# Prompt attention of a hybrid decoder step: scores computed transposed, four heads at a time, with the row maximum from a separate one-pass product

## The chip, the core and the metric

The kernel runs on one core of one Trainium2 chip. The metric is the device time of one execution in microseconds (us), the median of several runs. Engines are named as the profile names them: PE is TensorE (matrix products), PEld its weight loads, DVE VectorE, ACT ScalarE, POOL GpSimd, SP the queue that issues most DMAs.

## What is computed

One layer of a decoder is run for a prompt of 1024 tokens and for 8 requests of one new token each. The part that changes is the prompt's attention with three branches. There are 8 heads of 64 values, in 2 groups of 4 heads that share keys and values; queries are handled in blocks of 128.

```python
def masked_softmax(s, mask):
    s = jnp.where(mask, s.astype(jnp.float32), NEG)
    m = jnp.max(s, axis=-1, keepdims=True)
    p = jnp.where(mask, jnp.exp(s - m), 0.0)
    return p / jnp.maximum(jnp.sum(p, axis=-1, keepdims=True), 1e-30)
...
s = jnp.einsum('bqgrd,bngd->bqgrn', qg, kv_cmp[:, :, 0]).astype(jnp.float32) * ATTN_SCALE
s = s - slopes[:, :, None] * dist[None, :, None, None, :]
...
o = g[..., 0:1] * o_c + g[..., 1:2] * o_s + g[..., 2:3] * o_w
```

Each branch is scores, a distance term with a slope for each head, a mask, a softmax, and a product with the values. Branch 0 (selected) sees all earlier tokens, since with 1024 tokens all 16 blocks are selected. Branch 1 (window) sees the last 512. Branch 2 (compressed) sees 63 summary positions. The three outputs are added with sigmoid gates.

## The kernel before

The program is one hand-written stream for each engine, with semaphores between them. The order on PE is: input turned and projected (to 169 us), prompt attention (169.7 to 468.4 us), decode attention, recurrence, merge, and the feed-forward part, which takes half the time. Nothing else is on PE during the prompt attention, so that stage lies in the span as a whole.

Products of queries and keys are done with split operands (a high part and a low part in the type fp32r) so that they come near to full precision. One product over 128 rows takes the high keys twice against high and low queries (`k_high_twice`, `q_high_low`, L1008), a second over 65 rows takes the low keys against the high queries and the slope against the positions (L1010).

The stage is 128 jobs `j`: for each pair of heads, each block of queries `i` (0 to 7), and for `wc` 0 (selected) or 1 (window and compressed), each of the two heads. In a job:

- PE `scores`: queries are the weights and keys move, up to 512 columns at a time, so that the result has one query in each partition. Masks are added by a product of the identity and a bf16 mask (L1012, L1019).
- DVE `maxima` (L2029, L2035) takes the negated maximum over the row; ACT `exp` (L1634, L1640) takes the exponential with it as bias and sums the row in the same pass.
- PE `turn` (L1036) turns the probabilities, 128 keys at a time; ACT (L1666) and DVE `second` (L2067) copy them out of the accumulator memory.
- PE `pv` (L1056), for both heads of a pair in turn: the values are the weights, 64 columns wide, one head in each half of the array, and 128 probabilities move. The operands are plain fp32, which the trace records as two instructions for each product.
- ACT `parts` (L1648), PE `turn_parts` (L1065), DVE `scaled_sum` (L2053, L2055), PE `turn_sum` (L1070) and ACT `out` (L1653) scale by gate over sum, add the branches and turn the result back.

Four banks of the accumulator memory hold scores, two hold turned probabilities, and two hold outputs.

## Time and profile before

| | |
|---|---|
| median of 3 runs | 2190.33 us (2186.76 to 2195.27) |
| profiled execution, first to last instruction | 2191.0 us |
| PE busy | 2114.1 us, 96% of the span |
| DVE busy | 1035.5 us, 47% |
| ACT busy | 703.1 us, 32% |
| prompt attention (first L1008 to the last ACT copy) | 169.7 to 468.4 us, 298.7 us |

The profiled execution and the median agree within 0.7 us. Busy time counts an instruction from its start to its modelled end, so that overlapping products count once; the view of the chain of work shows what each one adds.

### The profile page before, as it was taken

How to read it: one execution, taken by the hardware profiler on the slowest of the kernel's cores; microseconds unless marked ns; L12 is line 12 of the kernel's file. 1: busy time of each engine (PE TensorE's matmuls, PEld its weight loads, DVE VectorE, ACT ScalarE, POOL GpSimd, SP SyncE). 2: the span in 40 equal slices, each digit the busy share in tenths (PEclk: the TensorE clock that was granted, in tenths of full speed). 3: DMA queues.
4: the chain of work that ended last, by engine and by line, in shares of the span. 5: the costliest groups of instructions: out<-in, count | busy, mean ns of one | idle time of the engine just before them, and what ended most of it. 6: DMA issues, size and time to landing. Idle time of an engine off the chain costs nothing.

```text
span 2191.0 us, 33624 instructions
## 1 busy us (share of the span) xinstructions
PE 2114.1 (96%) x14200; PEld 1827.4 (83%) x14200; DVE 1035.5 (47%) x1889; ACT 703.1 (32%) x1358; POOL 162.9 (7%) x164
## 2 busy tenths in 40 slices
PE   8999999989979999999999999999999999999997
PEld 7997777758639999999888886789888998889985
DVE  2136666636442466767221225644444344444447
ACT  3226677735431344444111112121111122111222
POOL 0021000001110122221000000000000000000007
PEclk9998999999999999999999999999999999999999
DMA  9322000135573222221321204121111111111101
GB/s 225 109 71 104 11 2 11 49 124 198 180 252 108 49 61 59 57 61 42 106 58 30 58 20 135 39 86 40 49 39 50 48 48 49 39 39 58 39 20 78
DMA packets 140626, 158.91 MB, mean 73 GB/s; under 512 B 25842, under 2 KB 122315, under 8 KB 135612
## 3 DMA queue, kind: packets, MB, share of 16 engines
q1 hardware_dynamic: 132444, 113.98, 17.3%
q0 software_dynamic: 8032, 42.78, 6.3%
q8 instruction: 113, 1.85, 0.3%
q14 instruction: 37, 0.30, 0.0%
HBM read 141.16 MB, written 19.76 MB: 73 GB/s over the span
## 4 chain that ended last, share of the span: by engine, by line
PE 89%; DMA 3%; DVE 3%; ACT 2%; issue 1%; SPq 0%; DVEq 0%; ACTq 0%; POOLq 0%
PE PS L834 62%; PE PS L1423 5%; PE PS L1056 3%; PE PS L1036 3%; PE PS L1139 3%; DMA arena<-in_cache_sel_kv,arena 2%; PE PS L1008 2%; PE PS L1010 1%; PE PS L1124 1%; PE PS L1349 1%; PE PS L1515 1%; PE PS L1065 1%; DMA arena<-in_x_prompt 1%; PE PS L1477 1%; PE PS L1292 1%
## 5 line engine op out<-in xcount | busy, mean ns | idle before, releaser
L834 PE MATMUL PS<-x_low,w_high_mlp 128*128 128x344 f32 x1056 | 338.1, 320 | 0.0
L834 PE MATMUL PS<-w_down_high,hidden 128*128 128x512 f32 x960 | 308.2, 395 | 0.9 <-DVE w_down_low L2547 0.9
L834 PE MATMUL PS<-x_high,w_low 128*128 128x344 f32 x768 | 246.1, 320 | 0.0
L2541 DVE TENSOR_TENSOR arena<-arena,PS 128x512 f32<-128x512 f32 x244 | 167.4, 687 | 134.9 <-PE PS L834 134.7
L834 PE MATMUL PS<-x_high,w_high_mlp 128*128 128x344 f32 x720 | 230.3, 320 | 0.0
L834 PEld LDWEIGHTS PS<-w_down_high,hidden 128*128 128x128 f32 x960 | 180.1, 188 | 54.3 <-DVE arena L2541 12.0
L834 PE MATMUL PS<-w_down_low,hidden 128*128 128x512 f32 x512 | 200.9, 392 | 0.0
L834 PEld LDWEIGHTS PS<-x_low,w_high_mlp 128*128 128x128 f32 x1056 | 198.6, 188 | 2.7
L834 PE MATMUL PS<-x_low,w_high_hgrn 128*128 128x344 f32 x600 | 192.6, 321 | 0.0
L834 PE MATMUL PS<-x_high_a,w_low 128*128 128x344 f32 x480 | 154.1, 321 | 0.0
L834 PE MATMUL PS<-x_high_b,w_low 128*128 128x344 f32 x468 | 149.7, 320 | 0.0
L834 PEld LDWEIGHTS PS<-x_high,w_low 128*128 128x128 f32 x768 | 144.5, 188 | 0.0
L834 PEld LDWEIGHTS PS<-x_high,w_high_mlp 128*128 128x128 f32 x720 | 135.8, 189 | 2.1 <-issue 1.5
L1576 ACT ACTIVATE arena<-PS 128x344 f32<-128x344 f32 (+1 forms) x105 | 47.9, 458 | 265.3 <-PE PS L834 265.2
L1893 ACT ACTIVATE w_down_high<-arena 128x2048 fp32r<-128x2048 f32 x15 | 28.7, 1916 | 275.2 <-PE PS L834 275.2
L1423 PE MATMUL PS<-arena,wring 128*128 128x344 f32 x384 | 114.7, 452 | 1.2 <-issue 1.2
L834 PEld LDWEIGHTS PS<-x_low,w_high_hgrn 128*128 128x128 f32 x600 | 113.8, 190 | 0.0
L834 PEld LDWEIGHTS PS<-w_down_low,hidden 128*128 128x128 f32 x512 | 96.1, 188 | 21.1
L858 DVE TENSOR_TENSOR w_low<-wring,w_high_mlp 128x1024 fp32r<-128x1024 f32 x44 | 53.6, 1219 | 108.9 <-ACT w_high_mlp L852 108.9
L834 PE MATMUL PS<-x_high_a,w_high_hgrn 128*128 128x344 f32 x300 | 102.0, 340 | 1.3 <-DMA x_high_b<-x_high_kept 1.3
L2701 POOL TENSOR_TENSOR arena<-arena 128x1024 f32<-128x1024 f32 (+1 forms) x8 | 19.6, 2451 | 1102.8 <-ACT arena L1905 1102.8
L1423 PEld LDWEIGHTS PS<-arena,wring 128*128 128x128 f32 x384 | 72.1, 190 | 35.1 <-issue 1.4
(390 smaller groups left out, 4285.0 us busy)
## 6 DMA issues: line engine op xcount, KB each, us to landing
wring<-in_w_in SPq DMA_DIRECT2D x100, 256.0 KB, 3.4
wring<-in_w_up SPq DMA_DIRECT2D x64, 256.0 KB, 3.2
arena<-in_w_down SPq DMA_DIRECT2D x16, 1024.0 KB, 5.0
arena<-in_x_prompt SPq DMA_DIRECT2D x16, 512.0 KB, 3.9
x_high_kept<-x_high_att SPq DMA_DIRECT2D x1, 4128.0 KB, 14.4
arena<-in_cache_win_kv SPq DMA_DIRECT2D x8, 512.0 KB, 4.5
arena<-in_w_out SPq DMA_DIRECT2D x2, 2048.0 KB, 8.8
out<-in_cache_win_kv SPq DMA_DIRECT2D x1, 4088.0 KB
```

What stands on the lines that cost most here:

```text
L834: mm = pe.matmul(out, w, x, start=(start and k == 0 and i == 0), stop=(stop and k == tiles - 1 and i == 2))
L858: dve.tensor_tensor(wl[:, n % WR, :, 0:m], wring[:, n % WR, :, 0:m], high[:, :, 0:m].bitcast(F32), ALU.subtract).then_inc(wl_dve, 1)
L1008: pe.matmul(out, qa, k1[g][:, br, k0:k0 + n], start=True, stop=False)
L1010: mm = pe.matmul(out, qb, k2[br][g][0:65, k0:k0 + n], start=False, stop=True)
L1036: mm = pe.transpose(PS[0:n, 4 + turned % 2, P * b:P * (b + 1)], probs(j, col, n), ident)
L1056: mm = pe.matmul(PS[HD * two:HD * (two + 1), 6 + i % 2, c:c + P], v[0:r, :], PT[(2 * n + two) % 3][0:r, b // 4, P * (b % 4):P * (b % 4 + 1 ...
L1065: mm = pe.transpose(PS[:, 6 + n % 2, P * a:P * (a + 1)], out_parts(n)[:, P * a:P * (a + 1)], ident)
L1139: mm = pe.matmul(PS[:, 4 + 2 * (b % 2) + c, 0:256], cw2[:, c, 4 * half + q, :], xt2[:, n % 2, 256 * (4 * c + q):256 * (4 * c + q + 1)], st ...
L1423: mm = pe.matmul(PS[:, product_bank(s, ab), 0:cn], wring[:, n % WR, 4 * ab + k, :], a[:, k, c0:c0 + cn], start=(k == 0), stop=(k == 3))
L1576: act.activation(dst[0:m, c0:c0 + cn], unit_out(3 * n + ci, m, cn), fn).then_inc(u_act, 1)
L1893: act.activation(wdh[:, :, :], wdn[:, g % 2], ACT.Copy).then_inc(wdh_act, 1)
L2541: dve.tensor_tensor(y, y, PS[:, 5 + d % 3, :], ALU.add).then_inc(dn_dve, 1)
```

## The change

The stage becomes 16 jobs `n`, one for each group of four heads and block of queries; the second group takes the blocks from 7 down to 0. A job has one step for each block of keys: `i + 1` selected, up to 5 window, 1 compressed, which makes 148 steps in all. In a step:

- PE `scores(n, x)`: 128 keys are the weights and the queries of four heads move, 512 columns, so that the result has one key in each partition. Two fp32r products as before (128 rows, and 68 rows that hold the low queries against the high keys, the slope and the three negated maxima). Where a mask is needed, the mask is the weight and the identity moves four times (512 columns).
- ACT `exp(n, x)`: one exponential of 512 columns with no bias and no row sum, straight into the weights of the next product.
- PE `values(s)`, two steps behind: for each head, the 128 x 128 probabilities are the weights, and 64 values and a column of ones move, 65 columns. The last column gives the row sum.

The maximum must be known ahead of the scores. `bound_scores(n + 1, p)` computes the next job's scores once more in the old layout, with one fp32r product over 65 rows (high parts alone) and the old masks, in 8 to 16 pieces, which take turns in two banks; DVE `bound` reduces each piece; PE `turn_max` turns the maxima and ACT `max_rows` puts them in as three rows of the queries. The pieces are spread over the steps of job `n`, all but the last two. After a job DVE `branch_sum` does sums, gates and the sum over branches in five steps, and PE `turn_out` turns it with two transposes.

The transposes of probabilities (`turn`), their copies (L1666, L2067), `parts` and `turn_parts` are gone. POOL sets ones, zeros and slopes ahead of the stage. The values are stored in rows of 65, and go out in four DMAs in place of two. The DMA that keeps the output runs once for each group (2 in place of 4).

```diff
+        def keys(n):
+            i = job(n)[1]
+            return [(0, b) for b in range(i + 1)] + [(1, b) for b in range(max(0, i - 4), i + 1)] + [(2, 0)]
...
+        def pieces(n):
+            i = job(n)[1]
+            w, lo = P * (i + 1), P * max(0, i - 4)
+            if i < 3:
+                return [[(0, 0, w, 0)], [(1, 0, w, 0), (2, 0, NCMP_P, w)]]
+            if i == 3:
+                return [[(0, 0, 512, 0)], [(1, 0, 512, 0)], [(2, 0, NCMP_P, 0)]]
+            return [[(0, 0, 512, 0)], [(0, 512, w - 512, 0)], [(1, lo, 512, 0)], [(1, lo + 512, P, 0), (2, 0, NCMP_P, P)]]
...
+        def pieces_at(n, x):
...
+            steps, total = len(keys(n)) - 2, 4 * len(pieces(n + 1))
+            return range(total * min(x, steps) // steps, total * min(x + 1, steps) // steps)
...
+            def bound_scores(n, p):
+                g, i = job(n)
+                hh, piece = p // len(pieces(n)), pieces(n)[p % len(pieces(n))]
+                x = first_piece[n] + p
...
+                if x >= 2:
+                    pe.wait_ge(sp_dve, x - 1)
+                q = q3[n % 2][0:HD + 1, P * hh:P * (hh + 1)]
+                for br, k0, w, col in piece:
+                    k = kc2[0:HD + 1, g, :] if br == 2 else k2[br][g][0:HD + 1, k0:k0 + w]
+                    mm = pe.matmul(PS[:, x % 2, col:col + w], q, k, start=True, stop=True)
...
+                        mm = pe.matmul(PS[:, x % 2, c:c + m.shape[1]], mask("ident"), m, start=False, stop=True,
...
+                mm.then_inc(sp_ps, 1)
...
+            def turn_max(n):
+                pe.wait_ge(m_dve, n + 1)
+                ring_free("max", n)
+                for hh in range(4):
+                    mm = pe.transpose(PS[0:HD + 4, ring_bank("max", n), P * hh:P * (hh + 1)], mx[:, 4 * hh:4 * hh + HD + 4], ident)
+                mm.then_inc(rb_ps, 1)
...
+            def scores(n, x):
...
+                out = PS[:, ring_bank("scores", n, x), :]
+                if br == 2:
+                    ka, kb, r = kc1[:, g, :], kc2[0:HD + 4, g, :], NCMP_P
...
-                    pe.matmul(out, qa, k1[g][:, br, k0:k0 + n], start=True, stop=False)
...
-                    mm = pe.matmul(out, qb, k2[br][g][0:65, k0:k0 + n], start=False, stop=True)
...
-            def turn(j, gi):
...
-                    mm = pe.transpose(PS[0:n, 4 + turned % 2, P * b:P * (b + 1)], probs(j, col, n), ident)
...
-            def pv(n):
...
-                        mm = pe.matmul(PS[HD * two:HD * (two + 1), 6 + i % 2, c:c + P], v[0:r, :],
-                                       PT[(2 * n + two) % 3][0:r, b // 4, P * (b % 4):P * (b % 4 + 1)],
...
+                    ka, kb, r = k1[g][:, br, P * b:P * (b + 1)], k2[br][g][0:HD + 4, P * b:P * (b + 1)], P
+                pe.matmul(out[0:r, :], ka, q1[n % 2][:, :], start=True, stop=False)
+                mm = pe.matmul(out[0:r, :], kb, q2[n % 2][0:HD + 4, :], start=False, stop=True)
+                m = mask("cmpmask", CMP_BACK - 8 * i) if br == 2 else mask("causal") if b == i else None
+                if br == 1 and b == i - 4:
+                    m = mask("winlow")
+                if m is not None:
+                    mm = pe.matmul(out.rearrange("p (h q) -> p h q", h=4), m, mask("ident").unsqueeze(1).to_broadcast([P, 4, P]),
+                                   start=False, stop=True, skip_group_check=True)
+                mm.then_inc(rb_ps, 1)
...
+            def values(s):
+                n, x = step_of[s]
+                g, i = job(n)
+                br, b = keys(n)[x]
+                pe.wait_ge(rb_act, ring["scores", n, x] + 1)
...
+                for hh in range(4):
+                    c = (HD + 2) * (3 * (hh % 2) + (br + 1) % 3)
+                    mm = pe.matmul(PS[:, 4 + 2 * (n % 2) + hh // 2, c:c + HD + 1], PT[:, s % 4, P * hh:P * (hh + 1)], v,
+                                   start=(x == 0 and hh % 2 == 0), stop=(br == 2 or b == i), skip_group_check=True)
...
+            for p in range(first_piece[1]):
+                bound_scores(0, p)
+            turn_max(0)
+            for n in range(NJ):
+                for x in range(len(keys(n))):
+                    scores(n, x)
+                    if n and x == out_step(n):
+                        turn_out(n - 1)
+                    for p in pieces_at(n, x):
+                        bound_scores(n + 1, p)
+                    if first_step[n] + x >= 2:
+                        values(first_step[n] + x - 2)
+                    if n + 1 < NJ and x == len(keys(n)) - 2:
+                        turn_max(n + 1)
+            for s in range(first_step[NJ] - 2, first_step[NJ]):
+                values(s)
+            turn_out(NJ - 1)
...
+            def max_rows(n):
+                act.wait_ge(rb_ps, ring["max", n] + 1)
+                act.activation(q2[n % 2][HD:HD + 4, :], PS[HD:HD + 4, ring_bank("max", n), :], ACT.Copy).then_inc(rb_act, 1)
+            def exp(n, x):
+                s, r = first_step[n] + x, NCMP_P if keys(n)[x][0] == 2 else P
+                act.wait_ge(rb_ps, ring["scores", n, x] + 1)
+                if s >= 4:
+                    act.wait_ge(pv_ps, s - 3)
+                act.activation(PT[0:r, s % 4, :], PS[0:r, ring_bank("scores", n, x), :], ACT.Exp).then_inc(rb_act, 1)
...
+                for at, (br, k0, w, col) in enumerate(piece):
+                    second = br < 2 and k0 == (512 if br == 0 else P * max(0, i - 4) + 512)
+                    dst = mx2[:, hh, br:br + 1] if second else mxr[:, hh, 1 + br:2 + br]
+                    ins = dve.tensor_reduce(dst, PS[:, x % 2, col:col + w], AX.X, ALU.max, negate=True)
...
+            def branch_sum(n):
...
+                dve.wait_ge(pv_ps, first_step[n + 1])
+                steps(dve.tensor_scalar(f, o[:, :, :, HD], 1e-30, None, ALU.max))
+                steps(dve.reciprocal(f, f))
+                steps(dve.tensor_tensor(f, f, gates[:, i, 12 * g:12 * g + 12].rearrange("p (a c) -> p a c", a=2), ALU.mult))
+                steps(dve.tensor_tensor(parts, o[:, :, :, 0:HD], f.unsqueeze(3).to_broadcast([P, 2, 6, HD]), ALU.mult))
+                dve.tensor_reduce(osum[:, n % 2, :, :], parts.rearrange("p a (t br) d -> p (a t) d br", br=3), AX.X, ALU.add
```

Where the instructions stand now. On PE, at the block of queries 6, before: two selected jobs of the pair, with the transposes between scores and products (each `L1056 64x128` row is one product, that is two instructions of the trace).

```order
L1008 MATMUL PS<-k_high_twice_54,q_high_low_61 128x512
L1010 MATMUL PS<-k_low_56,q_high_63 128x512
L1008 MATMUL PS<-k_high_twice_54,q_high_low_61 128x384
L1010 MATMUL PS<-k_low_56,q_high_63 128x384
L1012 MATMUL PS<-masks 128x128
L1036 MATMUL PS<-consts_sb,arena 128x128 x5
L1036 MATMUL PS<-consts_sb,arena 64x128
L1056 MATMUL PS<-arena 64x128 x12
```

On PE after, in job 6 (block 6 of the first group): three selected steps, with pieces of job 7 between `scores` (L1042, L1043) and `values` (L1064).

```order
L1042 MATMUL PS<-q_high_twice_61,k_high_low_53 128x512
L1043 MATMUL PS<-q_low_rows_65,k_high_rows_55 128x512
L1005 MATMUL PS<-k_high_rows_55,q_high_slope_64 128x512
L1064 MATMUL PS<-arena 128x65 x4
L1042 MATMUL PS<-q_high_twice_61,k_high_low_53 128x512
L1043 MATMUL PS<-q_low_rows_65,k_high_rows_55 128x512
L1005 MATMUL PS<-k_high_rows_55,q_high_slope_64 128x512
L1012 MATMUL PS<-masks 128x128
L1005 MATMUL PS<-k_high_rows_57,q_high_slope_64 128x512
L1012 MATMUL PS<-masks 128x128
L1064 MATMUL PS<-arena 128x65 x4
```

The transposes are gone from between the two kinds of product, the product with the values takes full-width weights, and the maximum's products stand in their place.

On PE after, at the start of the stage: the last piece of job 0, the turned maxima (L1024), the first scores, and the first pieces of job 1.

```order
L1005 MATMUL PS<-kc_high_rows,q_high_slope_63 128x64
L1012 MATMUL PS<-masks 128x64
L1024 MATMUL PS<-consts_sb,arena 68x128 x4
L1042 MATMUL PS<-q_high_twice_61,k_high_low_53 128x512
L1043 MATMUL PS<-q_low_rows_65,k_high_rows_55 128x512
L1048 MATMUL PS<-masks 128x512
L1005 MATMUL PS<-k_high_rows_55,q_high_slope_64 128x256
L1012 MATMUL PS<-masks 128x128
```

Before, the scores of the first five jobs stood here without a maximum ahead of them; now the first `scores` stand behind `turn_max(0)`, which waits for DVE and is followed by a copy on ACT.

On DVE before, in the same region of the stage: short reductions and copies by turns.

```order
L2029 TENSOR_REDUCE arena<-PS 128x1
L2035 TENSOR_REDUCE arena<-PS 128x1
L2067 COPY arena<-PS 128x384
L2043 RECIPROCAL arena<-arena 128x6
L2045 TENSOR_TENSOR arena<-arena 128x6
L2029 TENSOR_REDUCE arena<-PS 128x1
L2035 TENSOR_REDUCE arena<-PS 128x1
L2067 COPY arena<-PS 128x384
L2035 TENSOR_REDUCE arena<-PS 128x1
L2067 COPY arena<-PS 128x128
```

On DVE after, around the end of a job: the low queries (L1974), two or three reductions (L2010), then `branch_sum` (L2026 to L2030) and the reductions that PE's next pieces wait for.

```order
L1974 SCALAR_TENSOR_TENSOR q_low_rows_65<-arena,q_high_twice_61 64x2x128 x2
L2010 TENSOR_REDUCE arena<-PS 128x1 x3
L2026 TENSOR_SCALAR arena<-PS 128x12
L2027 RECIPROCAL arena<-arena 128x12
L2028 TENSOR_TENSOR arena<-arena 128x12
L2029 TENSOR_TENSOR arena<-PS,arena 128x768
L2030 TENSOR_REDUCE arena<-arena 128x256
```

The five instructions of `branch_sum` stand as one block between reductions; PE's pieces reuse their two banks only behind it.

## Rows read from the trace of the kernel before

**Rows 1.** The page: engines, and the chain that ended last by engine.
```profile
PE 2114.1 (96%) x14200; PEld 1827.4 (83%) x14200; DVE 1035.5 (47%) x1889; ACT 703.1 (32%) x1358; POOL 162.9 (7%) x164
...
PE 89%; DMA 3%; DVE 3%; ACT 2%; issue 1%; SPq 0%; DVEq 0%; ACTq 0%; POOLq 0%
```

**Rows 2.** Busy us of each engine by stretch, granted clock (PEclk), DMA share, GB/s.
```profile
core 0: us, PE busy (x) PEld busy (x) DVE busy (x) ACT busy (x) POOL busy (x), PEclk, DMA share, GB/s
...
169.70:188.00 18.30, 17.30 (x94) 13.02 (x95) 11.81 (x29) 12.52 (x46) 2.01 (x2) 0.56 0.58 218
188.00:462.00 274.00, 262.16 (x2513) 206.29 (x2513) 174.28 (x439) 194.75 (x577) 0.00 (x0) 0.99 0.05 18
```

**Rows 3.** What TensorE waited for from 169.7 to 468.4 us: total, times, longest.
```profile
PE PS L1056 <- ACT arena L1666: 4.5, 3, 1.5
...
PE PS L1036 <- ACT arena L1666: 0.3, 1, 0.3
```

**Rows 4.** TensorE by line and shape, same stretch: count, busy us, mean ns.
```profile
L1036 PE MATMUL PS<-consts_sb,arena 128*128 128x128 f32 x528 | 83.0, 283 | 1.8 <-DVE arena L2067 1.0 <-ACT arena L1666 0.3
L1056 PE MATMUL PS<-arena 128*64 128x128 f32 x1056 | 73.1, 282 | 6.6 <-ACT arena L1666 4.5 <-DVE arena L2067 1.3
L1008 PE MATMUL PS<-k_high_twice,q_high_low 128*128 128x512 f32 x88 | 42.9, 487 | 1.8 <-ACT arena L1640 1.8
```

**Rows 5.** Chain of work 278 to 285 us: start, us on the chain, what.
```profile
278.48 1.39 PE PS L1056 x20
279.87 0.43 PE PS L1008
280.30 0.24 PE PS L1010
280.54 0.07 PE PS L1012
280.61 0.12 PE PS L1008
...
281.00 0.11 PE PS L1018
...
281.15 0.58 PE PS L1036 x5
...
283.25 1.24 PE PS L1056 x20
```

**Rows 6.** The same chain at 1039 us, in the recurrence (full-width products, 64 columns).
```profile
1038.95 0.64 PE PS L834 x4
1039.59 0.84 PE PS L1292 x8
1040.43 0.53 PE PS L834 x3
1040.96 0.84 PE PS L1292 x8
```

**Rows 7.** The same chain at 770 us (8-column weights, 64 columns moved).
```profile
769.98 0.99 PE PS L1284 x16
```

**Rows 8.** VectorE by line and shape, 169 to 469 us (same columns).
```profile
L2055 DVE TENSOR_REDUCE arena<-arena 128x128 f32<-128x384 f32 x32 | 19.0, 594 | 1.1
L2053 DVE TENSOR_TENSOR arena<-PS,arena 128x384 f32<-128x384 f32 x32 | 17.8, 557 | 41.4 <-PE PS L1065 41.4
L2029 DVE TENSOR_REDUCE arena<-PS 128x1 f32<-128x64 f32 x64 | 14.1, 220 | 39.5 <-PE PS L1019 39.3
...
L2035 DVE TENSOR_REDUCE arena<-PS 128x1 f32<-128x512 f32 x16 | 11.0, 685 | 8.3 <-PE PS L1012 8.3
...
L2035 DVE TENSOR_REDUCE arena<-PS 128x1 f32<-128x256 f32 x16 | 6.6, 415 | 6.6 <-PE PS L1012 6.6
...
L2035 DVE TENSOR_REDUCE arena<-PS 128x1 f32<-128x128 f32 x16 | 4.3, 287 | 2.1 <-PE PS L1012 1.8
```

**Rows 9.** ScalarE by line and shape, 155 to 469 us (same columns).
```profile
L1666 ACT ACTIVATE arena<-PS 128x512 f32<-128x512 f32 x80 | 48.1, 601 | 57.7 <-PE PS L1036 57.3
```

586 lines of the change are left out of this document (243 added, 343 removed).

## The prediction

> **What bounds the kernel now.** I read the page first. PE is busy 96% of the span, and 89% of the chain that ended last is PE [rows 1]. PE is one in-order stream with nothing beside the prompt attention, so whatever this stage gains or loses on PE reaches the end. The stage is 298.7 us, from the first L1008 at 169.7 to the last copy at 468.4.
>
> Next, the stretches. From 188 to 462 us PE is busy 262 of 274 us, DVE 174, ACT 195 [rows 2]. So PE bounds the stage too, but 4% of it is idle, and both helpers have room. The first 18.3 us run at a granted clock of 0.56, nearly all of it at the lower of TensorE's two levels (1.2 GHz), although PE is busy 17.3 us of them [rows 2]. The granted clock fell after PE had waited for the last projection copy and the first maxima. The waits of PE in the stage have nine causes, from 4.5 us down to 0.3 us, together 14.5 us [rows 3].
>
> Busy time of overlapping products doesn't price them. The chain of work does: it shows what each adds. An fp32r product of 512 columns adds 0.23 us, one of 128 columns 0.12, one of 64 columns 0.11, a mask of 128 columns 0.07, a transpose 0.58 / 5 = 0.116 [rows 5]. A product with the values is two instructions in two halves of the array; two groups of 20 instructions take 1.39 and 1.24 us, so I take 0.066 each. Leaving the halved array costs too: the L1008 behind it adds 0.43 in place of 0.23 [rows 5].
>
> **Does this price list give the stage as it is?** Score products: each head has 11 spans of 512 columns, 3 of 384, 3 of 256, 7 of 128 and 8 compressed ones of 64, and each span is done twice. 88 x 0.233 + 24 x 0.18 (between its neighbours) + 24 x 0.12 + 56 x 0.12 + 64 x 0.11 = 41.4 us, twice 82.8. Masks 160 x 0.07 + 64 x 0.04 = 13.8. Transposes 592 x 0.116 = 68.7 (528 of them in [rows 4], the rest 64 columns wide). Value products 1184 x 0.066 = 77.9 (1056 of them in [rows 4]). Leaving the halves 64 x 0.17 = 11. Turning the outputs, 128 x 0.116 = 14.8. The sum is 269. With 14.5 of waits and 8 for the low clock (18.3 x 0.44) it is 292, against 298.7 measured: 2% short. The list can be used.
>
> **What the change removes.** All 592 transposes of probabilities (68.7 us), the old value products (77.9), leaving the halves (11), and 96 of the output transposes (11).
>
> **What it adds, on PE.**
> - Scores: 148 steps of two products of 512 columns, 296 x 0.233 = 69.0 us, in place of 82.8.
> - Score masks: in 56 steps, 512 columns. No row has this form; 0.07 for 128 columns and another 384 at the slope between 128 and 512 columns (0.113 for 384) gives 0.18, the sum of both ends at most 0.07 + 0.233 = 0.30. I take 0.24: 13.4 us.
> - The maximum's product: one of the two products of before, 41.4 us, with the old masks, 13.8 us.
> - Value products: 592, now with full-width weights and 65 columns moved, so 1184 instructions. This is the term that decides. The nearest row is L1292, a product of the same type with 128 x 128 weights and 64 columns: 8 instructions add 0.84 us, and the three L834 behind them add 0.53 where four add 0.64, 0.16 each, elsewhere; so (0.84 + 0.05) / 8 = 0.111 us each [rows 6]. L1284 moves the same 64 columns with 8-column weights at 0.99 / 16 = 0.062 [rows 7]. So it isn't the moved columns that cost 0.111; it is the full-width weights, loaded anew for each instruction. The new products load new probabilities each time. 1184 x 0.111 = 131.4 us. The bounds are 0.062 (73 us) and 0.116, a transpose (137 us).
> - Turned maxima and outputs: 96 x 0.116 = 11.1 us.
> - Narrow results: 16 compressed steps give 64 keys only. If each costs what the halves cost to enter and leave (up to 0.3), 5 us; nothing at the low end.
>
> The sum is 69.0 + 13.4 + 41.4 + 13.8 + 131.4 + 11.1 + 5 = 285. The same sum for before was 269. So what the 592 transposes and the halved products cost (158 us with leaving) nearly comes back as 131 for the new ones and 55 for the maximum. On PE work alone the change loses 16 us. It has to win that back from waits.
>
> The Trainium skill has a rule that speaks here: "TensorE: Matmul & The Clock Gate", section "LDWEIGHTS (loading the stationary operand)", says that a load takes its number of columns divided by 1.2 in ns, whatever the rows. For 128 columns that is 107 ns, and the trace's 0.111 agrees. By that rule swapping weights and moved operand trades a 64-column load for one of 128 columns that 65 moved columns can't cover.
>
> **What waits are left.** Today's waits (14.5) go with their instructions. New ones:
> - Start. Today the first scores run at once. Now eight pieces of job 0 go first, and DVE takes 4 x (0.287 + 0.287 + 0.220) = 3.2 us for them [rows 8] where PE needs 2.1. Then come a DVE step (0.2), the turn and its latency (0.3 over its price), and the copy of 512 columns on ACT, 0.6 [rows 9]. Job 0 has one step for the eight pieces of job 1: DVE 4 x (0.415 + 0.415 + 0.220) = 4.2 against 2.1 [rows 8]. That is about 4.5 us idle. The low clock stays, and does its harm to the PE work in it only: 6 us. Together 10 (bounds 8, as today, and 16 if the idle start keeps the clock low for longer).
> - Middle. DVE has 100 pieces for each group. Reductions sum to 114 us by their means (0.685 for 512 columns, 0.287 for 128 [rows 8]), `branch_sum` 16 x 2.5, of which its two large steps are 1.0 each (0.557 and 0.594 for half the columns [rows 8], and 0.4 more), low queries 16 x 0.7. Together 165 of 285 us: DVE isn't the bound. But `branch_sum` blocks it for 2.5 us, and PE can be two pieces ahead. A step of PE is 0.47 scores + 0.89 values + pieces. Where a step has 1.3 pieces (large blocks) PE meets the block after two steps, 3 us: hidden. Where it has 2.3 (jobs 2 to 4) it waits about 1 us. I take 5 us in all.
> - ACT: an exponential of 512 columns is 0.6 to 0.7, the copies of queries 0.7 more in the first two steps; a PE step is 1.4 or more, and PE reads the result two steps later. Hidden. If it weren't, each step would cost the difference.
> - End. `branch_sum` of the job before last stands in a job of three steps, and that of the last job has nothing ahead of it: 2.5 - 0.7, then 2.5, and a turn and a copy (0.9): 5 us.
>
> POOL's ones and slopes end before the projections do, and its larger DMAs leave during the stage, when the DMA share is 0.05 [rows 2]: nothing. If that cover were gone, the copies of 1 to 2 us would show at 169.7 us.
>
> Stage: 285 + 10 + 5 + 5 = 305, and 2 for the shortfall of the list: 307, that is 8 us more than 298.7. The profiled execution was 2191.0, the median 2190.3; so about 2199 us.
>
> **Rivals.**
> - Forecast: the stage is 299 to 313 us, the time 2190 to 2205. PE work as priced, waits of 14 to 28 us. Chance 0.50.
> - The pieces' two banks bind. There are 200 pieces, and each waits for the reduction two before it. PE to DVE and back costs some 0.1 to 0.2 us that no price holds, and if it shows on each piece, that is 20 us more, 2205 to 2222 (say 2218). For it: DVE is the slower side per piece (0.685 for 512 columns against 0.23 on PE). Against it: 1.4 us of other PE work lies between the pieces of large blocks. It decides once a piece's round trip is over the step. Chance 0.22.
> - Other side, mild: the waits vanish. The start is hidden behind the clock's return, DVE is never late, narrow results cost nothing. The stage is 280 to 292 us, 2172 to 2185. Against: today's deeper buffers still leave 14.5 us. It turns into a gain once start, middle and end together stay under 13 us. Chance 0.22.
> - Other side, large: the weight loads are hidden. If a new value product costs 0.062, as with narrow weights [rows 7], 1184 x 0.049 = 58 us go, 2141 us. For it: loads and products overlap elsewhere (the 344-column products, full width too, add 0.16 [rows 6]). Against: L1292 is the same form, and adds 0.111. The point at which the whole change breaks even is 0.104. Chance 0.06. The same page of the Trainium skill (section "Step-by-step: what each phase is for") has the next loads pulled ahead so that they run during a product; by that alone the product would cost its moved columns, as this rival has it, and rows 6 against rows 7 show that it doesn't for 64 columns.
>
> **Numbers.** Two runs of this kernel can't be told apart under 0.5%, 11 us: faster is below 2179.4, slower above 2201.3. Faster: 0.06 and 0.07 of the mild case, 0.13. Slower: 0.15 of the forecast and all of the second case, 0.37. Same: 0.50. The range holds the forecast, most of the second case and half of the mild one: 2180 to 2217. The forecast's own is 2190 to 2205.
>
> **What the profile after would show.** If I am right: L1064 adds 0.11 us an instruction on the chain, 131 us together; PE idle in the stage is 10 to 20 us, most of it at either end behind DVE L2010 and L2030; DVE is busy about 165 us there, ACT under 150; the granted clock is near 0.5 for the first 15 to 25 us of the stage and full behind. Wrong if L1064 adds 0.06 (large gain), if PE waits for L2010 throughout (loss of 20 us or more), or if a product of 512 columns with 68 rows, or the mask with a repeated identity, costs far from 0.23.

## The result, and the profile after

The changed kernel takes 2238.5 us (median of four runs; three at 2230.6 to 2242.7), the kernel before 2188.6 on the same chip: the ratio is 1.022, 95% interval 1.019 to 1.025. I had forecast 2199 (2180 to 2217), so the forecast was 40 us too low and the time is outside the range. The fourth run, at 2302.4 us with a mean granted clock of 0.941, is left out of the ratio, as two runs of one experiment (e6_nomax, 2187.7 and 2189.3 us) are. The median of the other three is 2234.3; below, an experiment is compared with this one, while the recorded expectations compare with 2238.5. The profiled execution took 2242.7, with a span of 2240.8.

The stage now reaches from 172.3 to 518.8 us: 346.5 us, 48 more than before. The windows of the changed kernel show where (the same columns as [rows 2]):

```profile
core 0: us, PE busy (x) PEld busy (x) DVE busy (x) ACT busy (x) POOL busy (x), PEclk, DMA share, GB/s
172.00:188.00 16.00, 12.99 (x61) 9.04 (x62) 7.08 (x27) 3.73 (x7) 8.70 (x14) 0.65 0.59 165
188.00:235.00 47.00, 41.04 (x256) 31.60 (x254) 26.91 (x70) 26.90 (x50) 0.00 (x0) 0.90 0.17 73
235.00:293.00 58.00, 58.00 (x232) 47.92 (x230) 18.36 (x41) 14.10 (x26) 2.02 (x2) 0.50 0.00 1
293.00:462.00 169.00, 166.72 (x1208) 139.49 (x1207) 82.64 (x189) 78.37 (x148) 0.00 (x0) 1.00 0.04 13
462.00:519.00 57.00, 51.05 (x366) 42.20 (x366) 26.44 (x70) 24.40 (x49) 0.00 (x0) 0.93 0.05 19
```

Look at the third row. For 58 us PE is busy all the time, at a granted clock of 0.50, which is the lower level of 1.2 GHz. It runs 232 products there, 4.0 in a microsecond; in the row behind, at the full clock, 1208 in 169 us, 7.1. Before, the clock was 0.99 from 188 to 462 us [rows 2]. The trace's record of the clock has the changed kernel at the lower level in four stretches up to the stage's end: from 177.0 for 13.7 us, from 217.9 for 6.8, from 235.0 for 58.0, and from 511.5 for 17.1. Before, it has them from 172.1 for 17.1 us, from 260.8 and from 332.5 for 3.4 each, and, just behind the stage, from 469.0 for 10.2. The two of 3.4 stand behind waits of 1.5 us for L1666, and a third wait of 1.5 us, at 404.7, has none behind it. So in the old stream a wait of this length cost little by the clock.

What PE waited for in the stage (total, times, longest):

```profile
PE PS L1005 <- DVE arena L2010: 9.0, 13, 2.1
PE PS L1072 <- DVE arena L2030: 4.9, 2, 2.8
PE PS L1042 <- ACT q_low_rows L1638: 0.9, 1, 0.9
PE PS L1024 <- DVE arena L2018: 0.7, 1, 0.7
PE PS L1005 <- ACT arena L1579: 0.5, 1, 0.5
PE PS L1107 <- ACTq L1675: 0.5, 1, 0.5
```

Together 16.5 us, against 14.5 in [rows 3]. The waits don't explain 48 us.

The chain of work of the changed kernel in three places: ahead of the long stretch (from 231 us), within it (253 us) and after it (330 us):

```profile
231.65 0.97 DVE arena L2029
232.62 0.02 issue
232.65 1.03 DVE arena L2030
233.68 0.61 DVE arena L2010
234.29 0.04 issue
234.33 0.50 PE PS L1005
234.83 1.35 PE PS L1064 x8
...
252.31 0.43 PE PS L1043
252.74 0.45 PE PS L1048
253.19 1.60 PE PS L1064 x8
254.80 0.53 PE PS L1042
...
330.65 0.89 PE PS L1064 x8
331.55 0.28 PE PS L1042
331.83 0.24 PE PS L1043
332.07 0.23 PE PS L1048
```

At the full clock eight value instructions add 0.89 us, 0.111 each, as priced. The mask of 512 columns (L1048) adds 0.23, priced 0.24. At the low clock each of these costs 1.8 to 2 times as much. Ahead of the stretch DVE does `branch_sum` (L2029 and L2030, 2.0 us) and only then the piece's maximum (L2010). PE waited 1.8 us for it and went on at 234.33. At 235.0 the clock fell. The fall at 217.9 stands behind a wait of 2.1 us that ended at 217.2, in which DVE did most of `decode_queries` (the queries of the decode part, 1.7 us), with a `branch_sum` just ahead of it.

**How much is clock, how much is work?** A run's span times its mean granted clock is about the time that it would take at the full clock throughout, since PE bounds nearly all of it; the rest, span x (1 - clock), is lost to the low clock. Before (seven runs beside the first experiments): clock 0.984 to 0.988, so 26 to 35 us lost and 2156 to 2159 without them. After: 0.968, 0.975 and 0.973, so 72, 56 and 60 us lost, and 2169 to 2177 without them. So 10 to 21 us of the loss are work and waits, where 8.7 were forecast, and the other 30 or so are the clock (63 us lost on average against 30).

### The profile page after: what moved, and what is told of

It is laid out like the page before. It is cut to its first block, busy times and chain, and to the rows that moved or that the text cites. A ratio compares the mean times of both kernels' runs of the same rounds, so it can differ in the third digit from the quotient of the medians.

```text
span 2240.8 us, 31835 instructions
## 1 busy us (share of the span) xinstructions
PE 2165.8 (97%) x13672; PEld 1882.4 (84%) x13672; DVE 1004.5 (45%) x1807; ACT 641.8 (29%) x1010; POOL 169.8 (8%) x178
## 4 chain that ended last, share of the span: by engine, by line
PE 91%; DVE 4%; DMA 3%; issue 1%; ACT 1%; SPq 0%; DVEq 0%; ACTq 0%; POOLq 0%
PE PS L841 60%; PE PS L1064 6%; PE PS L1426 5%; PE PS L1142 2%; PE PS L1005 2%; PE PS L1042 2%; DMA arena<-in_cache_sel_kv,arena 2%; PE PS L1043 2%; PE PS L1127 1%; PE PS L1352 1%; DVE arena L2010 1%; PE PS L1518 1%; PE PS L1048 1%; DMA arena<-in_x_prompt 1%; PE PS L1012 1%
## 5 line engine op out<-in xcount | busy, mean ns | idle before, releaser
L2010 DVE TENSOR_REDUCE arena<-PS 128x1 f32<-128x512 f32 (+4 forms) x256 | 104.3, 445 | 171.2 <-PE PS L1012 105.8
L1064 PE MATMUL PS<-arena 128*128 128x65 f32 x1184 | 170.9, 292 | 0.0
L1064 PEld LDWEIGHTS PS<-arena 128*128 128x128 f32 x1184 | 166.5, 212 | 2.9
L1645 ACT ACTIVATE arena<-PS 128x512 f32<-128x512 f32 (+1 forms) x148 | 88.3, 597 | 168.6 <-PE PS L1043 91.8
```

The costliest lines, as they stand in the source:

```text
L1064: mm = pe.matmul(PS[:, 4 + 2 * (n % 2) + hh // 2, c:c + HD + 1], PT[:, s % 4, P * hh:P * (hh + 1)], v, start=(x == 0 and hh % 2 == 0), sto ...
L1645: act.activation(PT[0:r, s % 4, :], PS[0:r, ring_bank("scores", n, x), :], ACT.Exp).then_inc(rb_act, 1)
L2010: ins = dve.tensor_reduce(dst, PS[:, x % 2, col:col + w], AX.X, ALU.max, negate=True)
```

## The experiments

Two theories at first. Both are about why the clock stays low while PE is busy. **Theory A**: PE's work in this stage moves few columns for the weights that it loads (65 columns for 128 loaded, twice over for each product), and where little moves, a low clock is held though PE is busy. **Theory B**: only the waits count; whatever makes PE wait for DVE costs the clock, and what the products look like is of no matter. Each wants an edit that leaves the other's cause as it is.

**e2_wide.** Each value product moves 128 columns (both groups' values) in place of 65. The weight loads and the number of instructions stay. What this kernel computes is no longer the prompt attention: columns of neighbours are added together, and the lower limit of the row sum is 1.0 in place of 1e-30.

```diff
-                v = vcN[:, g, :] if br == 2 else kvV[:, b, br, g, :]
+                v = (vcN if br == 2 else kvV[:, b, br, :, :]).rearrange("p g d -> p (g d)")[:, 0:128]
...
-                    mm = pe.matmul(PS[:, 4 + 2 * (n % 2) + hh // 2, c:c + HD + 1], PT[...], v,
+                    mm = pe.matmul(PS[:, 4 + 2 * (n % 2) + hh // 2, c:c + 128], PT[...], v,
```

> The changed kernel, but each value product moves 128 columns (64 values, ones, and the first 63 of the other group's) in place of 65; the attention output is not the reference's (neighbouring columns are added together, and the lower limit of the sum is 1.0). At the full clock it costs PE nothing if the full-width weight load bounds the product (0.111 us an instruction with 65 columns; 128 columns of a plain fp32 product add 0.11 too). Theory A (the low granted clock makes the loss, and few moved columns behind long weight loads hold it there): the 58 us stretch at the low clock with PE busy disappears or shrinks to under 20 us, the time falls by 15 to 35 us, to about 2205 to 2220. Theory B (waits for DVE start the low clock and nothing in the products holds it): the clock falls as before, same time within 10 us, 2230 to 2245. Theory C (the products bind by their moved columns): 30 us or more slower.

Measured: 2213.7 us, ratio to before 1.011 (1.008 to 1.014). Twice the columns, and 21 us faster. The waits for L2010 are as they were. The window from 200 to 450 us (columns as above), first of the changed kernel, then of this one:

```profile
200.00:450.00 250.00, 242.43 (x1534) 200.77 (x1532) 117.70 (x274) 106.91 (x199) 2.02 (x2) 0.87 0.03 13
```

```profile
200.00:450.00 250.00, 241.71 (x1730) 201.04 (x1730) 128.00 (x299) 119.78 (x224) 2.02 (x2) 0.99 0.03 10
```

Its PE waits for the maxima in the stage:

```profile
PE PS L1005 <- DVE arena L2010: 9.4, 14, 2.1
```

And a step of its chain of work:

```profile
303.16 0.95 PE PS L1064 x8
304.11 0.23 PE PS L1042
304.34 0.23 PE PS L1043
```

Two things follow. The granted clock is 0.99 where it was 0.87, with the waits unchanged: theory B alone falls. The same two waits are there, of 2.1 us (to 215.1) and 1.8 us (to 230.6); behind the first the clock is low for 3.4 us, behind the second not at all. And eight instructions with twice the columns add 0.95 with 0.23 behind them, in place of 0.89 and 0.28, the same sum to 0.01. The moved columns were hidden behind the weight loads: the price of 0.111 is that of the weights.

**e3_thin.** The same edit with 32 columns in place of 128, so that half of the values and the row sums are left out.

> The changed kernel, but each value product moves 32 columns in place of 65; the attention output is not the reference's (half the values and the sums are left out, and the lower limit of the sum is 1.0). Theory A: L1064 still adds 0.11 us an instruction at the full clock, the stretches at the low clock grow (over 80 us in the stage), and the time rises by 10 to 60 us, to 2245 to 2300. Theory B: no change, 2230 to 2245. Theory C: the products get cheaper by up to half, 50 us faster, about 2185.

Measured: 2430.6 us, ratio 1.112 (1.108 to 1.116): half the columns, 196 us slower. The clock is at the lower level for 491 us on end, from 196.3 to 687.8, nearly all of a stage that now lasts until 704. From 200 to 450 us PE is busy 249 of 250 us, and waits for L2010 are down to 1.9 us in the whole stage:

```profile
200.00:450.00 250.00, 249.15 (x968) 204.58 (x967) 79.23 (x185) 71.35 (x133) 2.02 (x2) 0.50 0.01 5
```

That is theory A at its clearest: PE busy 99.7% and the clock not given back. The stretch starts 2.5 us behind a wait of 0.45 us, at 193.8; the changed kernel has the same wait, at 198.3, and keeps its clock.

**e5_spread.** PE's program stays as changed; DVE's isn't. `branch_sum` is split over three steps, and `decode_queries`, `low_k` and ACT's copies of the second group's keys move to jobs with more steps.

```diff
-                    if x == 2 and n:
+                    if 2 <= x < 5 and n and len(keys(n)) > 5:
+                        branch_sum(n - 1, x - 2)
+                    if x == 2 and n and len(keys(n)) <= 5:
                         branch_sum(n - 1)
-                    if n == 2 and x == 3:
+                    if n == 5 and x == 5:
                         decode_queries()
```

> The changed kernel with DVE's work spread: the five steps of the branch sum stand in three consecutive steps of the job (where it has more than five), and the decode queries and the second group's low keys with their ACT copies are made in jobs 5 and 6 in place of 2 and 3. PE's stream is unchanged. Theory A and B both expect the waits of L1005 for L2010 to fall from 9 us to 4 or less. Theory B: the falls of the clock at 218 and 235 us are gone, the time falls by 25 to 40 us, to 2195 to 2212. Theory A: fewer falls, but one that does come is held as long; the time falls by 5 to 35 us. If only the waits count (theory D, DVE lateness is the whole loss), the time falls by about 5 us and the clock stays as it is.

Measured: 2211.5 us, ratio 1.010 (1.007 to 1.013), 23 us better than the changed kernel. The waits of PE for DVE in the stage fell from 9.0 to 2.9 us for the maxima, and rose from 4.9 to 7.5 behind the split sum (now L2033). Its 2.8 us stand at the end of the stage; between 190 and 470 us no wait is longer than 0.65 us:

```profile
PE PS L1072 <- DVE arena L2033: 7.5, 9, 2.8
PE PS L1005 <- DVE arena L2010: 2.9, 7, 0.7
```

And its window from 200 to 450 us:

```profile
200.00:450.00 250.00, 245.50 (x1776) 203.27 (x1775) 129.61 (x310) 124.27 (x233) 2.02 (x2) 1.00 0.03 10
```

That is 3.5 us less waiting, and span times clock is 2169, at the lower end of the changed kernel's 2169 to 2177. What went is the low clock in the middle: 1.00, where the changed kernel has 0.87 in the same window. So the falls at 218 and 235 us need their long waits. With the stream as changed a wait starts the fall, and the few moved columns make it last.

**e6_nomax.** The maximum's products, masks and reductions are left out, with a constant bound in place of the maximum, so that small probabilities vanish.

> The changed kernel without the maximum: bound_scores and its reductions are left out, and a constant stands for the negated maximum, so small probabilities vanish and the output is not the reference's. PE loses 55 us of products and masks by the price list, and the waits of L1005 for DVE (9 us). If the clock stays near full behind the start: 2170 + 0 - 55 - 10 + 20, about 2130 to 2150. If the low clock is held by the value products (theory A), their share of PE grows, and low stretches of 50 us or more remain: 2150 to 2185. Theory B: no waits, so no low clock behind the first 20 us: 2125 to 2140.

Measured: 2129.0 to 2142.1 us in three runs, ratio 0.976 (0.971 to 0.980); span times clock is 2100 to 2102. So the maximum costs about 68 us of the changed kernel's 2169. PE's own price was 41.4 + 13.8 = 55, and the 9.0 us of waits for the maxima went too; the 4 us left weren't looked for. The three runs lie where theory B had them (2125 to 2140, one run 2 us above), not where theory A had (2150 to 2185), at a clock of 0.982 to 0.988. So theory A's first form, in which value products of 65 columns hold the clock low whatever PE waits for, missed: even a stream in which they have a larger share can keep its clock where PE seldom waits. No trace shows the stage in these three runs.

**e7_both.** e5_spread and e2_wide together.

> Both edits together: DVE's sum over the branches is spread over three steps and its other long blocks are moved, and each value product moves 128 columns in place of 65 (so the output is not the reference's). Theory A (a fall of the clock needs a PE wait, and it lasts because value products move few columns behind full-width weights): either edit alone already took away the 65 us at the low clock in the middle of the stage, so together they don't add up; what is left of the low clock in the stage is its start and its end. The wide one alone gave 2213.7, the spread one alone 2211.5; together 2195 to 2207, since the waits (9.4 against 2.9 us) go as well. Rival (the two edits take away two different losses, 25 and 27 us): 2185 to 2190.

Measured: 2205.3 us, ratio 1.007 (1.005 to 1.009). The two gains (21 and 23 us) don't add up, since together they bring 29; in the main they take away the same loss. The clock is 0.983 to 0.986, near before's. What is left over before is 16.5 us, most of it the change's own cost in work and waits (span times clock is 2170 to 2173).

**e9_thin_more.** e3_thin, with the first score product of each step issued twice. A third theory stands against A here, **rival C**: the form of the value products alone decides, not what PE moves in all.

```diff
+                pe.matmul(out[0:r, :], ka, q1[n % 2][:, :], start=True, stop=True)
                 pe.matmul(out[0:r, :], ka, q1[n % 2][:, :], start=True, stop=False)
```

> The kernel whose value products move 32 columns in place of 65 (2430.6 us, clock held low for 491 us; the output is not the reference's), with more work: the first score product of each of the 148 steps (512 columns, fp32r, 0.233 us at the full clock) is issued twice, its first result overwritten. Added PE work 34 us at the full clock, 66 at the low. Theory A (the low clock is held where little moves behind the weight loads, so more moved columns let it come back): the clock returns, 2205 to 2250, that is about 200 us faster with 34 us more work. Rival C (what holds the clock is the value products' form or the stage itself, not what the engine moves in all): 2480 to 2500.

Measured: 2405.9 us, ratio 1.099 (1.097 to 1.101). More work, and 25 us faster than e3_thin, but the clock is still low for 324 us (from 240.3) and in three shorter stretches ahead of it. Both expectations missed in size, theory A's by over 150 us. The sign is theory A's: rival C wanted 50 us more.

**e8_r1 and e10_r1_wide.** Probabilities and values in fp32r (lower precision of this product), so that one instruction of 66 columns takes the place of two of 65; then the same with 128 columns (again with columns of neighbours added together).

```diff
-        PT = view(o, 4, 512); o += 4 * 512
+        PT = view(o, 4, 512)
+        PTr = rounded("probs_rounded", arena_at, o, 4, 512); o += 4 * 512
...
-                    mm = pe.matmul(PS[..., c:c + HD + 1], PT[:, s % 4, P * hh:P * (hh + 1)], v,
+                    mm = pe.matmul(PS[..., c:c + HD + 2], PTr[:, s % 4, P * hh:P * (hh + 1)], v,
```

> Probabilities and values stored as fp32r, so each value product is one instruction of 66 columns in place of two of 65 (592 in place of 1184). This lowers the precision of that product. It tests two terms: the price of a value product (0.111 us an instruction, by its weights), and the clock. If an fp32r value product also adds 0.11 us, 592 x 0.111 = 66 us go from the time without the low clock's loss (2169): 2103, and with the 30 us of loss at the stage's ends 2130 to 2145. Theory A by moved columns over time: a full step moves 1024 + 264 columns in about 0.90 us, more for each us than the changed kernel (1024 + 520 in 1.36), so the clock is held low no longer than there: 2130 to 2165. Rival C (what counts is the moved columns per weight load of the value products alone): low for most of the stage, 2250 to 2320.

> As the fp32r value products, but each moves 128 columns in place of 66 (the output is not the reference's). If the weight load sets the price of a value product, nothing is added, 0.11 us each: 2103 without loss, and with the loss at the ends 2130 to 2140, whichever theory of the clock holds. If the 66-column kernel is at 2130 to 2145 too, moved columns of the value products matter neither to price nor clock there; if it is far slower and this one isn't, rival C holds.

Measured: 2295.3 us (1.048, 1.046 to 1.050) with 66 columns, 2221.0 (1.016, 1.012 to 1.021) with 128. Removing 592 instructions made the kernel 61 us slower. Span times clock fell from 2169 to 2093, that is 0.128 us for each instruction removed (0.111 for itself, the rest for what stood around it). But the clock is low for 341 us on end, from 211.0. Rival C had this time right (2250 to 2320), and theory A had not (2130 to 2165). Doubling the columns gives 74 us back, which is rival C's way too, and the low stretches are then 7 to 21 us long, though there are many: its clock is 0.945 to 0.956, below the changed kernel's. The window of e8_r1 from 200 to 450 us:

```profile
200.00:450.00 250.00, 245.64 (x914) 189.18 (x912) 99.62 (x230) 89.40 (x166) 2.03 (x2) 0.52 0.03 9
```

The same window of e10_r1_wide:

```profile
200.00:450.00 250.00, 233.96 (x1170) 176.97 (x1168) 121.83 (x288) 114.00 (x216) 2.02 (x2) 0.75 0.03 9
```

My reading of theory A for e8_r1 was wrong: I had counted its moved columns as if fp32 and fp32r instructions were alike, and by this count it moves more in each microsecond than the changed kernel. It behaves as if it moved less. The trace of before has the time for a plain fp32 instruction of 256 columns with full-width weights, in the decode part:

```profile
499.92 3.47 PE PS L1139 x16
```

That is 0.217 us each, 0.85 ns a column, where an fp32r product of 512 columns takes 0.23 [rows 5], 0.45 ns a column. So an fp32 instruction occupies PE nearly twice as long for each column, and 128 of them, as in e2_wide, last just as long as the load (0.11). If fp32 columns are counted twice, the changed kernel moves slightly more than e8_r1, and the order of the kernels fits in the main, though not throughout (see the table). That the clock goes by such a count is an inference; no run tests it apart.

**e11_r1_more.** e8_r1 with the first score product of each step issued twice.

> The kernel with fp32r value products of 66 columns (2295.3 us, held at the low clock for 341 us; value products at fp32r precision), with more work: the first score product of each step (512 columns) is issued twice, its first result overwritten: 148 x 0.233 = 34 us more at the full clock, 66 more at the low one. Theory A, as the last runs left it: the low clock is held where columns move in too small a part of the time, each fp32 instruction counting its columns twice; the stream then stands between the fp32r kernel with 66 columns (held 341 us) and the one with 128 (2221.0, held 10 to 20 us at a time). So the clock comes back from time to time, and the kernel gets faster by work that it doesn't need: 2180 to 2250. Rival C (the value products alone decide): 2330 to 2360.

Measured: 2239.0 us, ratio 1.020 (1.015 to 1.025): 148 needless products of 512 columns make the kernel 56 us faster. Span times clock rose by 47 (34 were priced, so this measure is off by some 10 us where the clock is low for long), and the clock rose from 0.907 to 0.915 up to 0.955 to 0.967. Rival C, by which the value products alone decide, falls: they are the same here, and it wanted 2330 to 2360. Its window from 200 to 450 us, beside e8_r1's 0.52:

```profile
200.00:450.00 250.00, 241.59 (x1132) 185.53 (x1130) 109.74 (x258) 99.44 (x185) 2.02 (x2) 0.72 0.03 9
```

**e12_r1_spread.** e8_r1 with e5_spread's program for DVE.

> The fp32r kernel with the spread sum and the moved blocks on DVE, so with few PE waits (value products at fp32r precision). Its time without the low clock's loss is 2093. Theory B (the clock falls only behind a wait of PE, however little moves): it stays full from about 190 us on, 2115 to 2130, which would be faster than before by 3%. Theory A' (where little enough moves the clock falls and stays low by itself, waits or not): 2260 to 2300, hardly changed. The kernel with 32 columns had few waits left and was held for 491 us, so I hold A' for likelier.

Measured: 2288.3 us, ratio 1.045 (1.041 to 1.048), 7 us from e8_r1. The waits for the maxima are down to 2.7 us, six times, longest 0.8, and the clock is low all the same: for 95.6 us from 211.8, behind the wait of 0.8, and for 228.7 us from 317.6, behind one of 1.6 us for the last step of the sum. Those two waits, and then the window from 200 to 450 us:

```profile
PE PS L1006 <- DVE arena L2011: 2.7, 6, 0.8
PE PS L1073 <- DVE arena L2034: 1.6, 1, 1.6
```

```profile
200.00:450.00 250.00, 246.64 (x939) 188.33 (x938) 100.16 (x234) 93.80 (x174) 2.02 (x2) 0.54 0.03 9
```

So spreading DVE's work helps only a stream that can keep the clock. Where less moves, a small wait is enough. A fall with no wait of PE at all isn't shown: each long stretch in these traces starts within 3 us of one.

**e14_swap and e15_swap_late.** If few moved columns behind full-width weights are what costs, twice over, the operands should be swapped: the 65 columns of values are the weights, and the 512 columns of probabilities of all four heads move. One fp32r instruction for each step; ACT copies each finished branch, PE turns it, and the sum reads the turned parts. DVE's work is spread as in e5_spread.

```diff
-                for hh in range(4):
-                    c = (HD + 2) * (3 * (hh % 2) + (br + 1) % 3)
-                    mm = pe.matmul(PS[:, 4 + 2 * (n % 2) + hh // 2, c:c + HD + 1], PT[:, s % 4, P * hh:P * (hh + 1)], v,
+                pe.matmul(PS[0:HD + 1, 4 + a % 2, :], v, PTr[:, s % 4, :], start=first, stop=ends(s) is not None).then_inc(pv_ps, 1)
+
+            def turn_branch(a):
...
+                for hh in range(4):
+                    c = (HD + 2) * (3 * (hh % 2) + (br + 1) % 3)
+                    mm = pe.transpose(PS[:, 6 + hh // 2, c:c + HD + 1], acc[:, a % 2, P * hh:P * (hh + 1)], ident[0:HD + 1, 0:HD + 1])
```

> Operands of the value product swapped: the 65 columns of values and ones are the weights and the 512 columns of probabilities of all four heads move, fp32r (its precision is lower), one instruction of 0.233 us for each step in place of eight of 0.111; ACT copies each finished branch (48 copies of 512 columns), PE turns it in four transposes (192 x 0.116 = 22 us), and the sum over branches reads the turned parts. DVE's blocks are spread and moved as before. Sum for the value products: 148 x 0.233 + 22 = 57 us against 131 (and 5 for narrow results), so 2169 - 79 = 2090 without the low clock's loss. Theory A: nearly all of the stage moves 512 columns for each load of weights, so the clock is low only at its start and end, 2112 to 2135. Rival (the copies and turns bring waits of PE for ACT, some 0.4 us in each of 48): 2135 to 2155. If the clock is held in spite of 512-column products, theory A falls: above 2200.

Measured: 2168.3 us, ratio 0.990 (0.986 to 0.994): faster than before by 1%, with an fp32r product where before has fp32. The chain has the products at their price, 0.23 each, and the turns at 0.24 to 0.25 for four, half of what I took:

```profile
304.25 0.24 PE PS L1054
304.49 0.23 PE PS L1059
304.73 0.23 PE PS L1075
...
310.76 0.24 PE PS L1084 x4
```

What PE waits for most in its stage:

```profile
PE PS L1091 <- DVE arena L2071: 13.8, 11, 2.4
PE PS L1016 <- DVE arena L2048: 7.2, 17, 0.8
```

It missed its 2112 to 2135, and the rival's 2135 to 2155 too. PE's work is shorter, DVE's isn't, and the turned outputs (L1091) waited for the sum 11 times. Span times clock is 2104 to 2114, and the clock, at 0.969 to 0.978, fell behind the waits, though for 3 to 27 us at a time. The longest, 27.3 us from 192.9, stands behind a wait of 0.45 us only, and neither theory has it. e15_swap_late issues the turned outputs two steps later.

> The swapped value products (2168.3 us; waits of PE for the sum's L2071 13.8 us in 11 places, and seven falls of the clock to the low level between 233 and 445 us), with the turned outputs of the job before issued two steps later, behind which PE no longer waits in the larger jobs. If each wait goes and nothing takes its place: 8 to 11 us less waiting, and by theory A, which puts a fall behind a wait of PE where columns move densely, also fewer falls (they cost about 25 us in the middle of that stage): 2140 to 2158. If only the waits count and the falls stay: 2157 to 2162. If DVE is simply too slow for the shorter stage (its 178 us of work in 285), the wait moves to the pieces (L1016 behind L2048): 2165 to 2170.

Measured: 2162.2 us, ratio 0.989 (0.985 to 0.993). The waits for L2071 at L1091 went from 13.8 to 4.3 us, those for the maxima rose from 7.2 to 9.0, and of the hoped for 10 to 28 us it brought 6, within the noise of e14. Its time is at the edge of the middle reading (2157 to 2162), and the part of the waits that moved to the pieces is as the third had it. What PE waits for in its stage:

```profile
PE PS L1016 <- DVE arena L2048: 9.0, 24, 0.8
...
PE PS L1091 <- DVE arena L2071: 4.3, 3, 2.4
```

**All together**, roughly by how much moves in the stage beside the weight loads. The last column is the longest stretch at the lower level that began between 190 and 450 us.

| Kernel | value instructions for a step | median us | clock of the runs | longest, us |
|---|---|---|---|---|
| e3_thin | 8 fp32 of 32 columns | 2430.6 | 0.879 to 0.886 | 491.5 |
| e9_thin_more | the same, one score product more | 2405.9 | 0.911 to 0.914 | 324.3 |
| e8_r1 | 4 fp32r of 66 | 2295.3 | 0.907 to 0.915 | 341.3 |
| e12_r1_spread | the same, fewer waits | 2288.3 | 0.909 to 0.919 | 228.7 |
| e11_r1_more | as e8_r1, one score product more | 2239.0 | 0.955 to 0.967 | 75.1 |
| changed kernel | 8 fp32 of 65 | 2234.3 | 0.968 to 0.975 | 58.0 |
| e5_spread | the same, no long waits | 2211.5 | 0.980 to 0.985 | none |
| e10_r1_wide | 4 fp32r of 128 | 2221.0 | 0.945 to 0.956 | 20.5 |
| e14_swap | 1 fp32r of 512 | 2168.3 | 0.969 to 0.978 | 27.3 |
| e15_swap_late | the same, fewer long waits | 2162.2 | 0.967 to 0.974 | 27.3 |
| e2_wide | 8 fp32 of 128 | 2213.7 | 0.983 to 0.986 | 3.4 |
| e7_both | the same, no long waits | 2205.3 | 0.983 to 0.986 | none |

In the main the length of a stretch follows what moves, and how often one starts follows the waits. Three pairs don't keep the order of columns moved per microsecond, with fp32 columns counted twice: e9_thin_more moves less than e8_r1 and e11_r1_more more than the changed kernel, though their longest stretches say the reverse, and e14_swap moves more than e10_r1_wide with a longer one. Each length is from one trace. One value product less or more would hardly have told this; the kernels that do useless work and get faster do.

## Why the prediction was wrong

**The step that failed** is the start of the wait account: "The low clock stays, and does its harm to the PE work in it only: 6 us", and with it "the granted clock is near 0.5 for the first 15 to 25 us of the stage and full behind". The first part holds: the low clock lasts until 190.7 us, 18 us into the stage. "Full behind" doesn't. The clock falls three times more, at 217.9 (6.8 us), 235.0 (58.0) and 511.5 (17.1, of which 7.3 in the stage). At half speed these 72 us hold 36 us of loss; before, the two stretches of 3.4 us behind the start held 3.4. The forecast is 39.5 short of the median of all four runs, and 35 short of that of the three. I treated the clock as a thing of the stage's start, since [rows 2] had it at 0.99 for the rest. But that was a property of the old stream, and the change rewrote the stream. The price list, with its value products of 65 columns in 0.111 us that are all weight load, had what was needed to ask the question. The 2.1 us wait that started the first of these falls was not in the sum either: `decode_queries` isn't named in the prediction's account of DVE.

**PE's work was priced rightly.** L1064 adds 0.89 for eight, 0.111 each; L1048 0.23 (0.24 priced); products of 68 rows 0.24. Taking half of each kernel's low-clock stretches out of its stage (24 us of before, 86 of after) leaves 287 and 303.5 us; the forecast's 307 less its 6 for the clock is 301. With e7_both, where the clock is near before's, the whole kernel is 16.5 us over before, against 8.7 forecast. Small terms missed: the list fell short of the stage before by 7 us, and only 2 were added for it. Behind the value products L1042 adds 0.28 in place of 0.23, about 7 us in 148 steps that weren't priced (with e2_wide it adds 0.23, and the value products so much more). Narrow results, priced at 5 us, cost nothing: in the compressed step of the last job but one L1042 and L1043 add what they add elsewhere.

```profile
502.20 0.23 PE PS L1042
502.43 0.24 PE PS L1043
```

**The rival "weight loads are hidden" is out**, and e2_wide shows why: columns can be added for nothing, so the loads are what lasts. The forecast's break-even of 0.104 stands on the right side of 0.111.

**The waits** are 16.5 us, where the forecast had 14 to 28, and in the main where it put them: 4.9 us behind `branch_sum`, both at the end of the stage, and 9.0 for the pieces, 6.4 of them ahead of 240 us, in the small jobs. DVE is busy 161 us (165 forecast), ACT 148 (under 150). **The rival of the two banks** had a price of 20 us, and only 13 of 200 pieces waited: out as well, although the time went to its side and beyond its 2205 to 2222. It would be wrong to count this case for it.

**What each wait cost was wrong.** I priced a wait of 2 us at 2 us. In this stream the wait at 234.3 us cost 1.8 and then 29 more, by the clock. e5_spread shows it: 3.5 us of waits went, and 23 us came back.

The Trainium skill, "TensorE: Matmul & The Clock Gate", Part 1 on the clock gate, has the clock released by a busy engine and taken back by an idle one, so that work alone restores it. By that rule the 58 us and the 491 us at the lower level with PE busy throughout couldn't be; the measurements decide here.

**What stays open.** Which quantity the chip looks at wasn't found; that fp32 columns count twice for the clock is inferred from their time. What ends a stretch isn't shown either. A fall at the end of the stage (469 us before, 511 after) is in every kernel; after, it stands behind the wait of 2.1 us for L2030 that ended at 510.2, and no experiment took that wait away.

## What to carry to other kernels

When a change rewrites what TensorE runs for hundreds of microseconds, take the clock as a term of its own: ask how many columns each weight load carries, and what a wait of 2 us would cost if the clock fell behind it and stayed low. A PE busy share near 100% is no sign of health; read the granted clock beside it, and compare span times clock between kernels before looking for waits; where the clock is low for hundreds of microseconds, this measure was off by some 10 us here. And if a product is all weight load, let the wide operand move: here the swapped form took 0.23 us for a step in place of 0.89, and the two versions with it are the only ones with the whole computation that beat the kernel before, by 1%, at fp32r precision in that product.

## What the runs showed of the hardware that I had not expected

- A granted clock of 0.50 for 491 us with PE busy throughout (e3_thin), and for 341 us (e8_r1).
- Needless products can pay: 148 more of 512 columns took e8_r1 from 2295.3 to 2239.0 us, and e3_thin from 2430.6 to 2405.9. Twice the columns in each value product took the changed kernel from 2234.3 to 2213.7.
- 592 fewer instructions, 61 us more time (e8_r1 against the changed kernel).
- Eight fp32 instructions with 128-column weights and the score product behind them take 1.17 us with 65 moved columns and 1.18 with 128.
- A plain fp32 instruction takes 0.85 ns a column (0.217 us for 256), an fp32r product 0.45 (0.23 us for 512).
